# A hybrid SSD / HGRN2 / MoE layer on one core: an output-clearing store issued earlier, and the last pass's matmuls in another order

## The chip, the cores and the metric

The kernel runs on one core of one Trainium2 chip. Its time is the device time of one execution, in microseconds (us). TensorE (PE), VectorE (DVE), ScalarE (ACT) and GpSimd (POOL) compute; SyncE (SP) runs nearly all transfers of the stages looked at here from one queue, in the order in which its program issues them.

## The reference

One layer of a diffusion backbone on 512 latent and 256 context tokens of width 1024, in float32. Cut to the parts that the change lies in:

```
mixed = sigmoid(gm) * (ys @ w_branch_ssm) + sigmoid(gh) * (oh @ w_branch_hg)    # "merge"
mix   = mixed @ w_out
xl    = xl + gt1 * rms_norm(mix, g_post_mix)
h     = rms_norm(xl, g_pre_ffn) * (1 + sc2) + sh2
...                                # top-1 of 4 groups, then top-2 of its 8 experts, for each token
y[t]  = sum over its two experts e:  w_e * ((silu(h @ w_gate[e]) * (h @ w_up[e])) @ w_down[e])
out   = xl + gt2 * rms_norm(y, g_post_ffn)
```

ys and oh are the outputs of the two token mixers (a Mamba-2 scan and an HGRN2 scan), which the kernel computes before all of this.

## The kernel before

The five engines run programs of their own, tied by semaphores. The work has stages in this order: the modulation of the inputs, the SSD mixer, the HGRN2 mixer, the merge, the routing, the experts. The order in each engine's program is written by hand; a `wait_ge` holds that engine, and all that stands behind it in its program, until a semaphore has reached a count.

**Merge.** A loop over eight column tiles j of 128. For each tile PE computes two gates (lines of `merge_gate`, L1352), the SSM branch (L1758, 16 matmuls of 128x512) and the HGRN2 branch (L1760, 8 matmuls). A float32 matmul shows as two MATMUL instructions in the profile. The weights of tile j are 2.5 MB in four loads (two of gates at L1702, L1703, L1704) into one of two buffers r = j % 2. For j of 2 and more, SP issues them in `load(j, r)` after `s_brp >= j - 1`, and behind them 2 MB of modulation weights (`terms`, L1694), from which DVE makes one row a tile (`modulation_terms`, L1906, L1908). PE begins a tile with

```python
pe.wait_ge(s_wm[r], t * 64 + 32 + 32 * r)
```

so all four loads of the tile must have landed. Each finished row goes to DRAM by a small store from ACT (L1838), and SP waits for that (`s_modst`, L1707) before it loads the next bias (L1697). `w_out`, 4 MB, is loaded at L1732, ahead of the loop.

**Clearing y_dram.** Each expert writes its rows by an indirect store to `y_dram` (1024 rows of 1024 floats, 4 MB), of which all rows are first set to zero: POOL clears a 128x1024 tile `no_rows` (L2055) after the first mixed tile, and SP sends it to all of `y_dram` in one store (L1739), which before stands behind the loop over tiles. The first expert weights wait for that store (L2329, `s_cleared`), since they overwrite `no_rows`.

**After the merge.** SP waits for the last tile and for its stored row (L2299), then loads vectors, `x` and the router's weights (from L2310), then the first experts' weights. PE multiplies by `w_out` (L1776) and turns and routes the tokens.

**Experts.** Passes of two experts with 64 token slots each: gate and up (`up`, L2537), a turn of the product (L2544), down (`down`, L2555), copied by DVE (L2682, L2683) and stored by POOL (L2413). Weights of 4 MB a chunk stream into four homes. The last pass is written out by itself. Its result isn't stored, but added on PE to what the earlier passes stored: SP loads `y_dram` back in two halves (L2394), `s_yl`; DVE adds each token's two rows for the four chunks cc of 128 tokens (L2700, L2701), `s_fa`; `stored_choices(cc)` (L2630) puts chunk cc into its two PSUM banks (2 matmuls, 4 instructions); and `last_choices(cc, hf)` (L2633) adds the last pass's rows from `yb[0]`. The weights of the down projection come in four parts, `down_part(f)` (L2642, 4 matmuls, 8 instructions). SP issues parts 0 and 1 ahead of the loads from `y_dram`, and parts 2 and 3 behind them (L2287). After the last part DVE and ACT copy the two banks of the down projection into `yb[0]` (L2705, L2505), and only then can `last_choices(0, 0)` begin. ACT and DVE then normalise the chunks one by one (L2508 to L2513, L2711, L2715), and SP stores them (L2401).

Of the kernel before, what the change touches and what calls it, by code (L numbers as in the profile page):

```python
# [14 lines left out]
P = 128  # L15
D = 1024
# [5 lines left out]
LCH = LAT // P  # L22
# [38 lines left out]
FT = FF // P  # L61
# [5 lines left out]
PASSES = STEPS + 1  # L67
# [39 lines left out]
def build(nc, x, c, ctx, c_ctx, w_ada, b_ada, g_pre_mix, g_post_mix, g_pre_ffn, g_post_ffn, w_in,  # L107
# [7 lines left out]
    with es:  # L115
# [3 lines left out]
        def sem(name):  # L119
            return es.enter_context(nc.semaphore(name))  # L120
# [1557 lines left out]
        y_dram = nc.dram_tensor("y_dram", (2 * LAT, D), F32, kind="Internal").ap()  # L1678

        no_rows = arena[:, 6144:6144 + D]  # L1680

        def merge_sync(sp):

            def gate_source(j, b):
                return w_in_t[:, :, bass.ds((OFF_GM, OFF_GH)[b] + j * P, P)]

            def ssm_source(j):
                return wbs_t[:, :, bass.ds(j * P, P)]

            def hg_source(j):  # L1690
                return wbh_t[:, :, bass.ds(j * P, P)]

            def terms(j):
                sp.dma_start(wada2, w_ada_t[:, :, bass.ds(2 * D + j * 512, 512)]).then_inc(s_aw, 16)  # L1694

            def bias(j):
                sp.dma_start(adaw[0:1, :], b_ada[:, bass.ds(2 * D + j * 512, 512)]).then_inc(s_ab, 16)  # L1697

            def load(j, r):
                sp.wait_ge(s_brp, j - 1)  # L1700
                for b in range(2):
                    sp.dma_start(wmg[r][:, 8 * b:8 * b + 8, :], gate_source(j, b)).then_inc(s_wm[r], 16)  # L1702
                sp.dma_start(wmb[r][:, 0:16, :], ssm_source(j)).then_inc(s_wm[r], 16)  # L1703
                sp.dma_start(wmb[r][:, 16:24, :], hg_source(j)).then_inc(s_wm[r], 16)  # L1704
                sp.wait_ge(s_ac, j)
                terms(j)
                sp.wait_ge(s_modst, 16 * j)  # L1707
                bias(j)

            last = 8 * (HH - 1)  # L1710
            for b in range(2):
                sp.wait_ge(s_pu, last + 2 + 2 * b)
                sp.dma_start(wmg[0][:, 8 * b:8 * b + 8, :], gate_source(0, b)).then_inc(s_wg1, 16)
            sp.wait_ge(s_pu, last + 6)
            sp.dma_start(wmb[0][:, 0:16, :], ssm_source(0)).then_inc(s_wm[0], 16)
            sp.wait_ge(s_pu, last + 7)
            terms(0)
            sp.wait_ge(s_pu, last + 8)
            sp.dma_start(wmb[0][:, 16:24, :], hg_source(0)).then_inc(s_wm[0], 16)
            sp.wait_ge(s_sg, 4 * HH - 2)  # L1720
            sp.dma_start(wmg[1][:, 0:8, :], gate_source(1, 0)).then_inc(s_wm[1], 16)
            sp.wait_ge(s_q, HH)
            sp.dma_start(wmg[1][:, 8:16, :], gate_source(1, 1)).then_inc(s_wm[1], 16)
            sp.wait_ge(s_kdT, START + HH)
            bias(0)
            sp.wait_ge(s_out, START + HH)
            sp.dma_start(wmb[1][:, 0:16, :], ssm_source(1)).then_inc(s_wm[1], 16)
            sp.dma_start(wmb[1][:, 16:24, :], hg_source(1)).then_inc(s_wm[1], 16)
            sp.wait_ge(s_ac, 1)
            terms(1)  # L1730
            sp.wait_ge(s_ohd, START + HH)
            sp.dma_start(wout, w_out[0].rearrange("(k p) n -> p k n", p=P)).then_inc(s_wout, 16)  # L1732
            sp.wait_ge(s_modst, 16)
            bias(1)
            with sp.Fori(1, KT // 2) as t:
                for r in range(2):
                    load(t * 2 + r, r)
            sp.wait_ge(s_iota, ROWS_CLEAR)
            sp.dma_start(y_dram.rearrange("(j p) d -> p j d", p=P),  # L1739
                         no_rows.unsqueeze(1).broadcast_to([P, 2 * LCH, D])).then_inc(s_cleared, 16)  # L1740

        def merge_tensor(pe):
            def pair(t, warm):
# [276 lines left out]
        s_iota = sem("index_rows_ready")  # L2020
# [7 lines left out]
        s_gu = sem("gated_ready")  # L2028
        s_gut = sem("gated_transposed")
        s_guc = sem("gated_columns_ready")  # L2030
        s_d = sem("down_projected")
# [7 lines left out]
        ROWS_CLEAR, INDEX_ROWS, ROWS_NUMBERED = 1, 2, 3  # L2039
        s_part = {1: [s_wg1, s_wout, s_xres], 2: [s_aw, s_ab, s_modst]}  # L2040
        PART_BASE = {1: [32, 16, 16], 2: [128, 128, 128]}
        s_cleared = s_gc
# [210 lines left out]
        def weights_of(chunk):  # L2253
            w = home(chunk).rearrange("p (u q) -> p u q", u=2)
            if chunk % 3 == 2:
                return [w[:, u, :].rearrange("p (k n) -> p k n", n=D) for u in range(2)]
            return [w[:, u, :].rearrange("p (k f) -> p k f", f=FF) for u in range(2)]
# [257 lines left out]
        def experts_tensor(pe):  # L2515
# [9 lines left out]
            def part_landed(kind, part):  # L2525
                if part:
                    pe.wait_ge(s_part[kind][part - 1], PART_BASE[kind][part - 1] + 32)
# [34 lines left out]
            for step in STEP:  # L2562
                p = FIRST_PASS[step]
# [38 lines left out]
            n = pe.value_load(npair[0:1, 0:1], min_val=1, max_val=NOV // 2 + 1)  # L2602
# [13 lines left out]
            for cc in range(LCH):  # L2616
                mm = pe.transpose(bank[7][:, cc * P:(cc + 1) * P], cT[:, cc, :], ident[:, :])
# [9 lines left out]
            def stored_choices(cc):  # L2627
                pe.wait_ge(s_fa, cc + 1)
                for hf in range(2):
                    pe.matmul(bank[OUT_BANK[cc][hf]][:, :], ident[:, :], ylc[:, cc, hf * 512:(hf + 1) * 512], start=True, stop=False)  # L2630

            def last_choices(cc, hf):
                pe.matmul(bank[OUT_BANK[cc][hf]][:, :], cS[:, cc * P:(cc + 1) * P], yb[0][:, hf * 512:(hf + 1) * 512],  # L2633
                          start=False, stop=True).then_inc(s_fp, 1)

            def down_part(f):
                part_landed(2, f)
                w = weights_of(FINAL + 2)
                for hf in range(2):
                    for u in range(2):  # L2640
                        cols = slice(u * SLOT, (u + 1) * SLOT)
                        mm = pe.matmul(bank[5 + hf][cols, :], guT[:, f, cols], w[u][:, f, hf * 512:(hf + 1) * 512],  # L2642
                                       start=(f == 0), stop=(f == FT - 1))
                return mm

            pe.wait_ge(s_guc, PASSES + n + 1)
            pe.wait_ge(s_yb, PASSES + n)
            pe.wait_ge(s_w[(FINAL + 2) % 4], landed(OVER + 1) + n * 32)
            down_part(0)
            down_part(1)  # L2650
            pe.wait_ge(s_gu, PASSES + n + 1)
            stored_choices(0)
            stored_choices(1)
            down_part(2)
            down_part(3).then_inc(s_d, 1)
            stored_choices(2)
            pe.wait_ge(s_yb, PASSES + n + 1)
            last_choices(0, 0)
            pe.wait_ge(s_guc, PASSES + n + 2)
# [61 lines left out]
        @block.sync  # L2721
        def _(sp):
            modulate_sync(sp)
            ssd_sync(sp)
            hg_sync(sp)
            merge_sync(sp)
            experts_sync(sp)
# [24 lines left out]
        @block.tensor  # L2752
        def _(pe):
            for s in (s_xp, s_zp, s_kv, s_yd, s_yo, s_yt, s_kdT, s_la, s_kvH, s_out):
                pe.sem_inc(s, START)
            modulate_tensor(pe)
            ssd_tensor(pe)
            hg_tensor(pe)
            merge_tensor(pe)
            route_tensor(pe)  # L2760
            experts_tensor(pe)
# [41 lines left out]
```

## Time and profile before

| | us |
|---|---|
| median of 3 runs | 1880.98 |
| lowest, highest | 1880.73, 1887.57 |
| the profiled execution, its own time | 1887.57 |
| its span, first to last instruction | 1885.8 |

Times in the profile count from the start of the span. Busy time of PE counts MATMULs; a busy PE may be at half its clock, which is the column PEclk (1.00 is 2.4 GHz, 0.50 is 1.2 GHz). DMA share is the mean busy share of 16 DMA engines. A merged row of the timeline has a start, a length, an engine, a line and a count of instructions; in square brackets stands the idle time before it, and what ended it.

### The profile page before, as it was taken

Reading aid. Unit: us, or ns where it says so; the run is one execution under the profiler, and the core shown is the slowest. Engines: PE = TensorE matmul, PEld = TensorE weight load, DVE = VectorE, ACT = ScalarE, POOL = GpSimd, SP = SyncE. Lnnn points to the kernel's source line nnn. Section 1 sums busy time; section 2 is a strip of 40 time slices with the busy share of each in tenths; the row PEclk is TensorE's granted clock in tenths of the full one; section 3 lists DMA queues with packets and bytes.
Section 4 is the critical chain, followed back from the end, with each engine's and each line's share of the span. In section 5 each row is a group of like instructions: output and inputs, shape, how many; then the busy total and the mean of one; then the engine's idle time right before and its main releaser. Section 6 shows DMA issues by size and latency. Waiting matters only on the chain.

```text
span 1885.8 us, 19064 instructions
## 1 busy us (share of the span) xinstructions
PE 1766.8 (94%) x7112; PEld 957.6 (51%) x7112; DVE 717.5 (38%) x1176; ACT 486.3 (26%) x853; POOL 395.1 (21%) x472
## 2 busy tenths in 40 slices
PE   5999999999999999999999999999888987988877
PEld 2555555655556777767776444444533332333332
DVE  4526446364467555645646411311340000000004
ACT  3221422314134344344442100001311010111012
POOL 2024142231445433344333000000000000010000
PEclk9999999999999999999999999999889989999999
DMA  7221323113221111111120853344669999999996
GB/s 298 94 83 51 112 67 130 50 45 97 78 71 34 45 45 44 44 44 33 46 94 27 293 175 100 120 170 140 266 270 419 429 431 430 428 376 429 430 426 248
DMA packets 153578, 340.06 MB, mean 180 GB/s; under 512 B 15318, under 2 KB 105647, under 8 KB 140714
## 3 DMA queue, kind: packets, MB, share of 16 engines
q1 hardware_dynamic: 135648, 315.26, 43.9%
q10 hardware_dynamic: 13114, 15.89, 2.5%
q0 software_dynamic: 4752, 8.05, 1.1%
q8 instruction: 41, 0.67, 0.1%
q14 instruction: 23, 0.19, 0.0%
HBM read 331.44 MB, written 16.99 MB: 185 GB/s over the span
## 4 chain that ended last, share of the span: by engine, by line
PE 84%; DMA 7%; issue 3%; DVE 3%; ACT 1%; SPq 1%; POOL 0%; DVEq 0%; POOLq 0%; ACTq 0%
PE bank L774 12%; PE bank L522 12%; PE bank L2537 9%; PE bank L815 6%; PE bank L2555 5%; PE bank L1758 5%; PE bank L527 5%; PE bank L1352 4%; DMA arena<-in_w_up_dram 3%; PE bank L1776 3%; PE bank L518 3%; PE bank L1760 3%; PE bank L1386 3%; DMA arena<-in_w_down_dram 2%; PE bank L859 2%
## 5 line engine op out<-in xcount | busy, mean ns | idle before, releaser
L774 PE MATMUL bank<-stay,arena 128*128 128x512 f32 (+1 forms) x704 | 240.0, 497 | 0.0
L2537 PE MATMUL bank<-arena 128*64 128x512 f32 x832 | 189.6, 613 | 18.8 <-DMA arena<-in_w_up_dram 8.9
L774 PEld LDWEIGHTS bank<-stay,arena 128*128 128x128 f32 x704 | 132.4, 190 | 99.7 <-issue 92.3
L522 PE MATMUL bank<-arena 128*128 128x512 f32 x384 | 168.9, 593 | 0.0
L1256 POOL TENSOR_TENSOR arena<-arena 128x256 f32<-128x256 f32 x112 | 87.8, 784 | 267.8 <-DVE arena L1509 153.7
L2555 PE MATMUL bank<-arena 128*64 128x512 f32 x416 | 105.7, 666 | 33.6 <-issue 15.8
L2537 PEld LDWEIGHTS bank<-arena 128*64 128x64 f32 x832 | 66.8, 141 | 137.0 <-issue 120.5
L815 PE MATMUL bank<-arena,stay 128*128 128x512 f32 x256 | 114.6, 596 | 3.0 <-DVE arena L1067 3.0
L522 PEld LDWEIGHTS bank<-arena 128*128 128x128 f32 x384 | 71.7, 190 | 83.7 <-issue 83.7
L2676 DVE TENSOR_TENSOR arena<-arena,bank 128x512 f32<-128x512 f32 x17 | 11.7, 687 | 238.9 <-PE bank L2537 238.9
L1528 DVE TENSOR_TENSOR arena<-arena 128x256 f32<-128x256 f32 x112 | 58.9, 566 | 104.5 <-ACT arena L1287 73.0
L1758 PE MATMUL bank<-stay,arena 128*128 128x512 f32 x224 | 97.4, 593 | 0.0
L2413 POOL DMA_INDIRECT y_dram<-arena x16 | 16.1, 1007 | 384.9 <-DVE arena L2683 384.3
L534 ACT COPY arena<-bank 128x512 f32<-128x512 f32 x64 | 32.4, 506 | 213.2 <-PE bank L522 93.7
L575 POOL TENSOR_TENSOR arena<-arena,tok 128x512 f32<-128x512 f32 x40 | 49.5, 1241 | 173.0 <-ACT arena L654 109.9
L2444 ACT ACTIVATE arena<-bank,arena 128x128 f32<-128x128 f32 x136 | 49.2, 467 | 137.5 <-PE bank L2522 136.2
L2555 PEld LDWEIGHTS bank<-arena 128*64 128x64 f32 x416 | 37.5, 151 | 92.8 <-issue 88.6
L1352 PE MATMUL bank<-stay,arena 128*128 128x512 f32 x192 | 84.0, 595 | 0.0
L2682 DVE COPY arena<-bank 128x512 f32<-128x512 f32 x16 | 11.1, 691 | 187.5 <-PE bank L2555 187.5
L1258 POOL TENSOR_TENSOR arena<-arena 128x256 f32<-128x256 f32 x112 | 80.5, 719 | 0.0
L815 PEld LDWEIGHTS bank<-arena,stay 128*128 128x128 f32 x256 | 47.3, 190 | 61.2 <-issue 51.7
L1922 DVE TENSOR_TENSOR stay<-stay,bank 128x512 f32<-128x512 f32 x8 | 5.5, 687 | 180.6 <-PE bank L1760 180.6
(432 smaller groups left out, 2733.0 us busy)
## 6 DMA issues: line engine op xcount, KB each, us to landing
arena<-in_w_gate_dram SPq DMA_DIRECT2D x24, 2048.0 KB, 17.7
arena<-in_w_down_dram SPq DMA_DIRECT2D x24, 2048.0 KB, 22.7
arena<-in_w_up_dram SPq DMA_DIRECT2D x22, 2048.0 KB, 22.2
arena<-in_w_in_dram SPq DMA_DIRECT2D x58, 512.0 KB, 3.8
arena<-in_w_ada_dram SPq DMA_DIRECT2D x12, 2048.0 KB, 10.3
stay<-in_w_gate_dram SPq DMA_DIRECT2D x8, 2048.0 KB, 21.4
stay<-in_w_up_dram SPq DMA_DIRECT2D x8, 2048.0 KB, 17.3
arena<-in_w_in_dram ACTq DMA_DIRECT2D x6, 2048.0 KB, 9.7
```

The lines of the kernel that those rows point to most:

```text
L518: mm = pe.matmul(b[:, 0:CTX], w[:, k, :], hT[:, k, LAT:T], start=(k == 0), stop=(k == KT - 1))
L522: mm = pe.matmul(b[:, :], w[:, k, :], src[:, k, 0:LAT], start=(k == 0), stop=(k == KT - 1))
L527: mm = pe.matmul(b[:, i * P:(i + 1) * P], lhs, w[:, k, :], start=(k == 0), stop=(k == KT - 1))
L774: mm = pe.matmul(ps[:, 0:n], w[:, k, :], hT[:, k, o:o + n], start=(k == 0), stop=(k == KT - 1))
L815: mm = pe.matmul(bank[z_bank(j)][:, :], hT[:, k, j * P:(j + 1) * P], wz[:, k, :], start=(k == 0), stop=(k == KT - 1))
L1256: pool.tensor_tensor(first[:, :, 0:half], one, two, ALU.subtract)
L1258: ins = pool.tensor_tensor(second[:, :, half:], one, two, ALU.subtract)
L1352: mm = pe.matmul(bank[4 * r + b][:, :], wmg[r][:, 8 * b + k, :], hT[:, k, 0:LAT], start=(k == 0), stop=(k == KT - 1))
L1528: own.mark(dve.tensor_tensor(wv[:, :, s], ev[:, :, s], level_view(kh[d], half)[:, :, s], ALU.mult))
L1758: pe.matmul(bank[4 * r + 2][:, :], wmb[r][:, k, :], ysT[:, k, :], start=(k == 0), stop=(k == 15))
L2537: mm = pe.matmul(b[cols, :], xgT[r][:, k, cols], w[u][:, k, :], start=(k == 0), stop=(k == KT - 1))
L2555: mm = pe.matmul(bank[5 + hf][cols, :], guT[:, f, cols], w[u][:, f, hf * 512:(hf + 1) * 512], start=(f == 0), stop=(f == FT - 1))
```

## The change

Two places. In `merge_sync` the store that clears `y_dram`, with its wait for `no_rows`, is issued before the loads of tiles 2 to 7 instead of behind them. In the last expert pass on PE, `stored_choices(0)` and `(1)` now come ahead of the first down part, `stored_choices(2)` comes between down part 0 and down part 1, and parts 1 to 3 follow one another.

```diff
             bias(1)
+            sp.wait_ge(s_iota, ROWS_CLEAR)
+            sp.dma_start(y_dram.rearrange("(j p) d -> p j d", p=P),
+                         no_rows.unsqueeze(1).broadcast_to([P, 2 * LCH, D])).then_inc(s_cleared, 16)
             with sp.Fori(1, KT // 2) as t:
                 for r in range(2):
                     load(t * 2 + r, r)
-            sp.wait_ge(s_iota, ROWS_CLEAR)
-            sp.dma_start(y_dram.rearrange("(j p) d -> p j d", p=P),
-                         no_rows.unsqueeze(1).broadcast_to([P, 2 * LCH, D])).then_inc(s_cleared, 16)
...
+            stored_choices(0)
+            pe.wait_ge(s_gu, PASSES + n + 1)
+            stored_choices(1)
             pe.wait_ge(s_guc, PASSES + n + 1)
             pe.wait_ge(s_yb, PASSES + n)
             pe.wait_ge(s_w[(FINAL + 2) % 4], landed(OVER + 1) + n * 32)
             down_part(0)
-            down_part(1)
-            pe.wait_ge(s_gu, PASSES + n + 1)
-            stored_choices(0)
-            stored_choices(1)
-            down_part(2)
-            down_part(3).then_inc(s_d, 1)
             stored_choices(2)
+            for f in range(1, FT):
+                mm = down_part(f)
+            mm.then_inc(s_d, 1)
             pe.wait_ge(s_yb, PASSES + n + 1)
             last_choices(0, 0)
```

## Rows read from the trace of the kernel before

**Rows 1.** Windows: share of PE, DVE, ACT, POOL, clock and DMA by stretch.

```profile
800.00:1000.00 200.00, 200.00 (x1057) 143.02 (x1057) 110.73 (x183) 83.78 (x121) 85.68 (x112) 1.00 0.20 58
1400.00:1500.00 100.00, 88.14 (x396) 36.13 (x396) 7.90 (x12) 15.28 (x39) 8.13 (x8) 0.93 1.00 425
```

**Rows 2.** The chain that ended last, merge and what follows it.

```profile
1075.86 13.93 PE bank L1352 x32
...
1280.92 6.88 PE bank L1760 x16
...
1290.76 27.70 PE bank L1776 x64
```

**Rows 3.** Timeline of SP's transfers in the merge.

```profile
1058.76 0.25 SPq L1697 DMA_DIRECT2D arena<-in_b_ada_dram  x1
1059.37 1.01 SPq L1702 DMA_DIRECT2D arena<-in_w_in_dram  x2
...
1061.68 2.88 SPq L1704 DMA_DIRECT2D arena<-in_w_branch_hg_dram  x1
...
1256.99 0.38 SPq L1739 DMA_DIRECT2D y_dram<-arena  x1
1291.98 0.36 SPq L2310 DMA_DIRECT2D stay<-modrows  x1
```

**Rows 4.** Timeline of POOL, where the tile of zeros is made.

```profile
1055.34 1.24 POOL L2055 MEMSET arena<- 128x1024 f32 x1 [32.60 <-DVE arena L1924]
```

**Rows 5.** Windows of 2 us: the last columns are PEclk, DMA share and GB/s.

```profile
1058.00:1060.00 2.00, 2.00 (x6) 0.95 (x5) 1.93 (x3) 0.00 (x0) 0.00 (x0) 1.00 0.28 111
1064.00:1066.00 2.00, 2.00 (x6) 0.95 (x5) 0.00 (x0) 0.00 (x0) 0.00 (x0) 1.00 1.15 347
1258.00:1260.00 2.00, 2.00 (x6) 0.95 (x5) 1.91 (x3) 0.00 (x0) 0.00 (x0) 1.00 1.02 422
1514.00:1516.00 2.00, 2.00 (x7) 0.64 (x5) 0.00 (x0) 0.00 (x0) 0.00 (x0) 0.53 0.98 418
```

**Rows 6.** Transfers: count, KB each, us from issue to landing.

```profile
y_dram<-arena SPq DMA_DIRECT2D x1, 4096.0 KB, 11.4
arena<-in_w_branch_hg_dram SPq DMA_DIRECT2D x8, 512.0 KB, 7.5
```

**Rows 7.** Timeline of PE in the last pass.

```profile
1851.45 0.72 PE L2544 MATMUL bank<-ident,arena 128*128 128x128 f32 x4 [0.95 <-DVE arena L2676]
1852.90 3.65 PE L2642 MATMUL bank<-stay,arena 128*64 128x512 f32 x16 [0.73 <-ACT arena L2454]
1857.95 3.88 PE L2630 MATMUL bank<-arena,ident 128*128 128x512 f32 x8 [1.39 <-DVE arena L2701]
1863.23 1.94 PE L2642 MATMUL bank<-stay,arena 128*64 128x512 f32 x8 [1.41 <-DMA stay<-in_w_down_dram]
1865.71 1.94 PE L2642 MATMUL bank<-stay,arena 128*64 128x512 f32 x8 [0.54 <-DMA stay<-in_w_down_dram]
1867.58 1.98 PE L2630 MATMUL bank<-arena,ident 128*128 128x512 f32 x4
1869.40 5.31 PE L2633 MATMUL bank<-arena,stay 128*128 128x512 f32 x12
```

**Rows 8.** Timeline of DVE in the last pass.

```profile
1858.50 1.28 DVE L2701 SCALAR_TENSOR_TENSOR arena<-arena 128x1024 f32<-128x1024 f32 x1
1861.55 1.28 DVE L2701 SCALAR_TENSOR_TENSOR arena<-arena 128x1024 f32<-128x1024 f32 x1
1867.70 0.69 DVE L2705 COPY arena<-bank 128x512 f32<-128x512 f32 x1 [2.89 <-PE bank L2642]
```

**Rows 9.** Timeline of PE in the passes: matmuls after an idle stretch.

```profile
1513.31 8.78 PE L2555 MATMUL bank<-arena 128*64 128x512 f32 x32 [2.98 <-ACT arena L2454]
1573.80 7.09 PE L2555 MATMUL bank<-arena 128*64 128x512 f32 x32 [2.98 <-ACT arena L2454]
1836.55 13.95 PE L2537 MATMUL bank<-arena 128*64 128x512 f32 x64 [2.55 <-ACT arena L2444]
```

## The prediction

> **What bounds the kernel now.** I read the windows first. Before the routing PE is the bound: in a stretch of two hundred microseconds of the mixers it is busy for all of them, DMA at 0.20 [rows 1]. In the experts the transfers are: share 1.00, 425 GB/s, PE at 88 of 100 us [rows 1]. So a delay that reaches PE before the experts delays the start of the weight stream, and with it the end, one for one; a delay inside the stream would be hidden; and one behind the last weights counts in full again. The change has one edit in the first kind of place, and one in the last.
>
> The chain that ended last shows the merge: from tile 2 (1075.86) to the end of tile 7 (1280.92 + 6.88 = 1287.80) it is PE alone, six tiles in 211.94 us, 35.3 us each, with no wait for a load in it [rows 2]. The reader is to see there that every microsecond in which PE waits for a tile's weights is a new one. Then SP's timeline: the store that clears y_dram goes at 1256.99, and SP's next transfer, held by the last tile, at 1291.98 [rows 3]. Last, the timelines of the final pass [rows 7, 8].
>
> **The store: what it is taken from.** It lands 11.4 us after its issue [rows 6], at 1268.4, and nothing is issued until 1291.98 [rows 3]: its cover is 23.6 us of empty queue. The first expert weights wait for it only after that. So taking it out there gives 0 us. If that cover were gone, it would give up to 11.4 us.
>
> **The store: what it is put in front of.** In the new place SP comes to it right after the bias load at 1058.76 [rows 3]. Its own wait is for the zeros, done at 1055.34 + 1.24 = 1056.58 [rows 4]: no new wait on SP. Its issue costs SP 0.38 us [rows 3]. What is queued behind it is the whole of tile 2: 2.5 MB of weights, issued from 1059.37 to 1061.68 + 2.88 [rows 3], then 2 MB of modulation weights. In the kernel before, the queue has just run dry there (share 0.28 in 1058 to 1060 [rows 5]), so tile 2's data start about 1060.5, run at 347 GB/s [rows 5] and are complete 7.5 us after the start of the last issue, 1061.68 + 7.5 = 1069.2 [rows 3, 6]. PE begins tile 2 at 1075.86 [rows 2]. So tile 2 has a slack of 6.7 us, and the store must fit into it.
>
> It does not. 4.19 MB at 422 GB/s, the rate of the same store where it stands now [rows 5], are 9.9 us. Starting about 1060.0, they leave the queue's engines free at about 1069.9, where tile 2's data would have started at 1060.5: a shift of 9.4 us. Tile 2 then lands at 1069.2 + 9.4 = 1078.6 and PE, ready at 1075.86, waits **2.7 us**. Bounds: if half of the 1.2 us between issue and first data overlaps, 2.1; if tile 2's data start only when the store has landed whole, 11.4 us after an issue at 1059.3, the shift is 1070.7 - 1059.4 = 11.3 and the wait 4.6 us. I take 2.7: a DMA share of 1.00 over 100 us of one load after another [rows 1] says that this queue goes from one transfer to the next without a gap.
>
> The Trainium skill (DMA: Bandwidth & Descriptors, "Specifications") gives an HBM limit of some 358 GB/s for a core; by it the store would take 11.7 us (an estimate from that page) and the wait would be 4.5 us. The store's own row, 422 GB/s, contradicts it here, and I go by the row.
>
> What else is behind the store: DVE's modulation row of tile 2 starts some 6 us later (its weights follow tile 2's on the queue), but PE wants it only at the end of tile 2, about 35 us on. SP may issue tile 3's loads when PE has done tile 1, about 1075.9; if they take the 9.8 us of tile 2's (1059.37 to 1069.2) they land near 1086 and are wanted at 1075.86 + 35.3 = 1111.2, so 9.4 us later is still early. So there is one stall, and by tile 3 the queue has caught up. What is late next is all that follows on PE: w_out's matmuls at 1290.76, the vectors at 1291.98, routing, the start of the stream. Nothing there has slack against PE, so 2.7 us pass to the end.
>
> Does the stall lower the clock? Rows 9 show what idling does: the same 32 instructions take 8.78 us after 2.98 us of idle time in one pass (clock 0.53 just behind it [rows 5]) and 7.09 in another, so a drop costs 1.7 us and comes after most but not all gaps near 3 us. The gap of 2.55 us left the next matmuls at full speed [rows 9]. For 2.7 us I expect no drop (0 us; the other end is 1.7).
>
> **The last pass on PE.** In the kernel before, down parts 0 and 1 run from 1852.90 for 3.65 us, while the rows from y_dram are still on their way; `stored_choices(0)` begins at 1857.95, when DVE has added the first chunk [rows 7]. Parts 2 and 3 wait for their weights, and part 3 begins at 1865.71 and ends at 1867.65. Then DVE and ACT copy for 0.69 us [rows 8], hidden under `stored_choices(2)` (1867.58, 1.98 us), and `last_choices(0, 0)` begins at 1869.40 [rows 7].
>
> After the change PE reaches `stored_choices(0)` at 1852.17 (1851.45 + 0.72) and stands behind it until 1857.95, because nothing about the rows from y_dram is earlier. The 3.65 us of parts 0 and 1 have lost their cover. From there PE is alone the bound, instruction by instruction. An instruction of 128x512 takes 0.43 us (1.94 us for 4 and their drain, of which about 0.22 is drain: 1.72), and one of a down part half of that (8 in 1.72), as two run side by side:
>
> - `stored_choices(0)`: 1857.95 to 1859.67
> - `stored_choices(1)`: its chunk is ready at 1858.50 + 1.28 = 1859.78 [rows 8], so 1859.88 to 1861.60
> - down part 0: to 1863.32
> - `stored_choices(2)`: its chunk is ready at 1862.83 [rows 8], so to 1865.04
> - down parts 1, 2, 3: 5.15 us to 1870.19, plus the drain, 1870.4. Part 3's weights are there from 1865.71 [rows 7], so it waits for none.
> - the copies of 0.69 us, now with nothing over them, and 0.2 us of hand-over: `last_choices(0, 0)` at **1871.3**, against 1869.40: 1.9 us later.
>
> From `last_choices(0, 0)` on nothing changes: ACT and DVE do the four chunks in the same order, and DVE sets the end.
>
> Then the clock. PE now idles from 1852.17 to 1857.95, 5.8 us, twice what in most passes was enough for a drop. At the full price of 1.7 us, of which some 0.2 goes into the wait for the second chunk that PE had anyway, this is 1.5 us. Ends: 0, and 2.9 (the 5.8 us gap could hold the low clock over more work: half of the whole wait). I take 1.5. The sum for the last pass is **3.4 us**, between 1.9 and 4.8.
>
> **Sum.** 0 + 2.7 + 0 + 1.9 + 1.5 = 6.1 us slower, bounds 2.1 + 1.9 = 4.0 and 4.6 + 1.7 + 4.8 = 11.1. Against the profiled execution's own 1887.57 us (span 1885.8, so 1.8 us around it) this is 1893.7. That execution was the slowest of the three; the same 6.1 us on the median of 1880.98 give **1887.1 us**, 0.32% slower. A measurement of this kernel tells about 0.5%, 9.4 us, from no change; the runs before alone spread over 6.8 us.
>
> **Rivals.**
>
> *A. Slower by more than 0.5%: tile 2 waits until the store has landed.* Place: the start of tile 2. It decides when loads behind a store in one queue wait for its completion, or when SP is held in issuing them. Then PE waits 4.6 us, a gap after which a clock drop is near certain, 1.7; with 3.4 in the last pass 9.7 us, 1890.7. Against it: the queue streams loads without gaps; for it: the trace shows no store with loads right behind it. Chance 0.15. The Trainium skill (same page, "Anatomy of one DMA") puts most of a fixed 2 us of a transfer into the receipt of its last write, longest for HBM; it says this of the semaphore, not of the data behind it, and no row here shows which holds.
>
> *B. Faster: the stored chunks fill waits.* The order pays if PE's work is done when part 3's weights arrive: `stored_choices(2)` would be out of the 1.98 us behind part 3 [rows 7], of which 0.9 is needed for copies anyway, so at most 1.1 us are won. PE has 5.15 us of down parts from 1865.04, and would have to begin them 2.8 us earlier, so the rows from y_dram would have to come 2.8 us earlier. With a hidden store the time would be 1879.9; with more than 0.5% faster only if the move of the store also frees something at 1292, where the queue is empty. Chance 0.04, most of it measurement.
>
> *C. The merge edit is hidden.* If the store and tile 2 share the engines better than first come, first served, or tile 2's slack is larger than 6.7 us, only the last pass pays: 3.4 us, 1884.4; without a clock drop 1.9, 1882.9. Chance 0.20.
>
> **Chances.** The forecast 0.61, A 0.15, B 0.04, C 0.20. The likeliest is 1887.1. The range takes C without a drop and a little of the spread below, and A with the upper bounds: 1881.0 to 1892.5. Of the forecast's cases one in ten crosses 9.4 us with the spread, of A's half or more: slower 0.17; faster 0.03; within 0.80.
>
> **What would show it.** In the profile after: the clearing store at about 1059.3; an idle gap of PE of 2 to 3 us ahead of L1352 of tile 2, released by a load; tiles 3 to 7 without one; nothing new between 1287 and 1320 but the shift; in the last pass an idle gap of 5 to 6 us ahead of the first L2630, a clock at 0.5 behind it, and 1.9 to 3.4 us more from the landing of the rows of y_dram to the first L2633. The forecast is wrong if that first gap isn't there, if it is over 4 us, or if the stream of weights swallows the delay.

## The result

| | before | after |
|---|---|---|
| median, us | 1880.86 (4 runs) | 1894.01 (4 runs) |
| lowest to highest | 1879.78 to 1887.57 | 1893.01 to 1895.22 |
| span of the profiled execution | 1885.8 | 1891.7 |

The ratio is 1.0062, with a 95% interval of 1.0038 to 1.0087: the change makes the kernel slower, by 13.2 us on these medians. Put on 1880.9 us, the ratio is 11.7 us and its interval 7.1 to 16.4. The forecast was 6.1 us slower, 1887.1 us, with a range up to 1892.5; the direction was right and the time lies outside.

SP's timeline of the kernel after, in the merge, answers to [rows 3]:

```profile
1057.26 0.24 SPq L1697 DMA_DIRECT2D arena<-in_b_ada_dram  x1
1057.55 0.37 SPq L1736 DMA_DIRECT2D y_dram<-arena  x1
1058.29 8.43 SPq L1702 DMA_DIRECT2D arena<-in_w_in_dram  x2
1066.91 3.10 SPq L1703 DMA_DIRECT2D arena<-in_w_branch_ssm_dram  x1
1070.10 2.88 SPq L1704 DMA_DIRECT2D arena<-in_w_branch_hg_dram  x1
```

The store is the transfer right behind the bias load, as forecast (at 1057.55, where 1059.3 was named). What is new is the second column: SP needs 8.43 us to issue two loads that took it 1.01 before [rows 3], and the last load of tile 2 is issued 12.6 us after the store. PE's timeline there, and the windows (PEclk, DMA share and GB/s last):

```profile
1073.49 1.02 PE L1766 MATMUL bank<-arena,ones 128*1 128x512 f32 x2
1077.85 15.67 PE L1352 MATMUL bank<-stay,arena 128*128 128x512 f32 x32 [3.35 <-DMA arena<-in_w_branch_hg_dram]
...
1115.00 14.00 PE L1352 MATMUL bank<-stay,arena 128*128 128x512 f32 x32
```

```profile
1068.00:1070.00 2.00, 2.00 (x6) 0.80 (x6) 0.00 (x0) 0.00 (x0) 0.00 (x0) 1.00 0.91 222
1070.00:1072.00 2.00, 2.00 (x6) 0.91 (x5) 0.00 (x0) 0.00 (x0) 0.00 (x0) 1.00 1.15 347
1080.00:1082.00 2.00, 2.00 (x4) 0.86 (x3) 0.00 (x0) 0.00 (x0) 0.00 (x0) 0.50 1.05 410
```

A new idle gap of 3.35 us stands ahead of tile 2, and the 32 instructions behind it take 15.67 us where tile 3's take 14.00: the clock is at 0.50, and that costs 1.7 us more. From tile 3 on nothing waits. In the chain that ended last, the gap ends with the landing of tile 2's last load, and SP's own issuing is a link ahead of it:

```profile
1066.91 3.10 SPq L1703
...
1070.10 7.52 DMA arena<-in_w_branch_hg_dram
...
1077.85 4.16 PE bank L1352 x6
```

A link in that chain doesn't say yet what SP's being held costs. For that I set the two profiles side by side, counted from SP's issue of the bias load. Tile 2's last load landed 10.42 us after it in before (1058.76 to 1069.18) and 20.36 us after it in after (1057.26 to 1070.10 + 7.52 = 1077.62): 9.9 us more, where the forecast had 9.4. So whatever the forecast lacked there, SP's being held included, costs 0.5 us in all.

Whether the loads wait for the store to land can be read from the packets: those of the store are of 4 KB, those of the loads under 2 KB. The first line is of the kernel before, for 1265.5 to 1267.5, two us near the end of its store. The other two are of the kernel after, for 1067 to 1069 and for 1069 to 1070.05, which is the moment at which the store has landed (1057.55 + 12.5):

```profile
DMA packets 208, 0.85 MB, mean 426 GB/s; under 512 B 0, under 2 KB 0, under 8 KB 208
```

```profile
DMA packets 136, 0.56 MB, mean 279 GB/s; under 512 B 0, under 2 KB 0, under 8 KB 136
DMA packets 416, 0.27 MB, mean 257 GB/s; under 512 B 16, under 2 KB 398, under 8 KB 416
```

The loads' packets run before the store has landed, so they don't wait for that. But with loads queued behind it the store's own last packets are slower (279 GB/s where it had 426), and it lands 12.5 us after its issue where it took 11.4. Why, no run here shows.

The last pass on PE answers to [rows 7], and DVE's row to [rows 8]:

```profile
1855.81 0.72 PE L2544 MATMUL bank<-ident,arena 128*128 128x128 f32 x4 [0.95 <-DVE arena L2676]
1859.08 6.25 PE L2630 MATMUL bank<-arena,ident 128*128 128x512 f32 x8 [2.55 <-DVE arena L2701]
1865.26 1.94 PE L2642 MATMUL bank<-stay,arena 128*64 128x512 f32 x8
1867.12 1.98 PE L2630 MATMUL bank<-arena,ident 128*128 128x512 f32 x4
1869.04 5.37 PE L2642 MATMUL bank<-stay,arena 128*64 128x512 f32 x24
1875.20 5.42 PE L2633 MATMUL bank<-arena,stay 128*128 128x512 f32 x12 [0.79 <-DVE arena L2705]
```

```profile
1856.95 0.75 DVE L2700 TENSOR_SCALAR arena<-arena 128x1024 f32<-128x1024 f32 x1 [1.29 <-DMA arena<-y_dram]
...
1874.46 0.69 DVE L2705 COPY arena<-bank 128x512 f32<-128x512 f32 x1 [8.43 <-PE bank L2642]
```

PE idles ahead of `stored_choices(0)`, whose instructions, eight together with those of `(1)`, then take 6.25 us (3.88 before), works through all down parts, and stands for the copies, 0.79 us, which lay under a matmul before.

To see what each stretch costs I cut every profiled execution at the same five starts: the first L1760 of the merge, the first L1776, the first L2537, the first L2700, the first L2633, and the end of the span (the lines shift by a few in some of the variants). Differences of these, in us, for all kernels that were run:

| kernel | up to the merge | merge | w_out, routing | experts | last pass | end | span |
|---|---|---|---|---|---|---|---|
| before | 1046.03 | 244.73 | 93.77 | 471.20 | 13.67 | 16.40 | 1885.8 |
| before again (e1) | 1042.34 | 244.74 | 93.86 | 469.47 | 13.73 | 16.36 | 1880.5 |
| after | 1044.67 | 249.82 | 92.36 | 470.10 | 18.25 | 16.50 | 1891.7 |
| e2 store only | 1043.51 | 250.75 | 93.82 | 471.85 | 13.67 | 16.40 | 1890.0 |
| e3 last pass only | 1043.44 | 244.73 | 93.88 | 470.29 | 17.40 | 16.46 | 1886.2 |
| e4 both | 1042.91 | 249.96 | 92.15 | 470.09 | 17.65 | 16.54 | 1889.3 |
| e5 two stores | 1045.50 | 260.82 | 92.15 | 469.82 | 13.66 | 16.45 | 1898.4 |
| e6 two halves | 1046.66 | 244.73 | 92.16 | 469.70 | 13.71 | 16.44 | 1883.4 |
| e7 behind tile 3 | 1045.08 | 244.73 | 92.18 | 470.15 | 13.67 | 16.39 | 1882.2 |
| e8 filled waits | 1045.55 | 248.46 | 93.83 | 470.61 | 17.91 | 16.54 | 1892.9 |
| e9 stored ahead | 1046.88 | 244.73 | 92.15 | 470.24 | 13.52 | 16.48 | 1884.0 |
| e10 parts late | 1044.94 | 244.73 | 93.90 | 469.65 | 14.87 | 16.41 | 1884.5 |

The merge and the last pass repeat to 0.1 us when nothing in them is changed. Those are the only two stretches in which after differs from before beyond what executions of one kernel differ by: +5.1 and +4.6 us, 9.7 in sum. What the change doesn't touch varies by itself: 1042.3 to 1046.9 up to the merge, 92.2 or 93.8 in the routing, 469.5 to 471.9 in the experts.

### The profile page after: what moved, and what is told of

Read it like the earlier page. It is cut to its first block, busy times and chain, and to the rows that moved or that the text cites. A ratio compares the mean times of both kernels' runs of the same rounds, so it can differ in the third digit from the quotient of the medians.

```text
span 1891.7 us, 19064 instructions
## 1 busy us (share of the span) xinstructions
PE 1771.4 (94%) x7112; PEld 959.5 (51%) x7112; DVE 717.3 (38%) x1176; ACT 486.6 (26%) x853; POOL 395.7 (21%) x472
## 4 chain that ended last, share of the span: by engine, by line
PE 84%; DMA 7%; issue 3%; DVE 3%; ACT 2%; SPq 1%; ACTq 0%; POOL 0%; DVEq 0%; POOLq 0%
PE bank L774 12%; PE bank L522 12%; PE bank L2537 9%; PE bank L815 6%; PE bank L2555 5%; PE bank L527 5%; PE bank L1352 5%; PE bank L1758 4%; PE bank L1776 3%; PE bank L518 3%; PE bank L1386 3%; PE bank L1760 3%; DMA stay<-in_w_up_dram 2%; DMA stay<-in_w_down_dram 2%; PE bank L859 2%
## 5 line engine op out<-in xcount | busy, mean ns | idle before, releaser
L2537 PE MATMUL bank<-arena 128*64 128x512 f32 x832 | 186.8, 606 | 15.2 <-ACT arena L2444 7.6
L2537 PEld LDWEIGHTS bank<-arena 128*64 128x64 f32 x832 | 66.2, 140 | 131.2 <-issue 118.0
L2676 DVE TENSOR_TENSOR arena<-arena,bank 128x512 f32<-128x512 f32 x17 | 11.7, 688 | 238.3 <-PE bank L2537 238.3
L1352 PE MATMUL bank<-stay,arena 128*128 128x512 f32 x192 | 85.7, 605 | 3.3 <-DMA arena<-in_w_branch_hg_dram 3.3
```

The costliest lines, as they stand in the source:

```text
L1352: mm = pe.matmul(bank[4 * r + b][:, :], wmg[r][:, 8 * b + k, :], hT[:, k, 0:LAT], start=(k == 0), stop=(k == KT - 1))
L2537: mm = pe.matmul(b[cols, :], xgT[r][:, k, cols], w[u][:, k, :], start=(k == 0), stop=(k == KT - 1))
```

## Experiments

**e1, the kernel before once more**, to see what its own executions do.

> The kernel before, unchanged. Theory: its profiled execution of 1887.57 us was not typical; a new one takes 1880 to 1882 us, and the 6 to 7 us less lie in the experts (from the start of the first expert pass at L2537 to the load of y_dram), not in the merge or the last pass. Rival: the 6.8 us are spread evenly or lie ahead of the merge, and then the profile of before can be used as it stands. Ratio to before 1.000, within 0.003.

Measured 1882.52 us (11 runs, 1880.22 to 1885.21) beside 1884.03 for 27 runs of before on the same chip (1880.17 to 1887.12); ratio 0.9994, 0.9985 to 1.0003. The expectation of where the difference sits was wrong: of the 5.3 us between the two spans 3.7 lie ahead of the merge and 1.7 in the experts. 1887 us isn't an odd execution but the upper end of a spread of 7 us. So the four runs of before with their median of 1880.86 were low for this kernel: 27, 23 and 23 runs of it in three later comparisons have medians of 1884.03, 1884.47 and 1884.64.

**e2, e3, e4: each edit alone, and both.** e2 takes only the hunk of `merge_sync`, e3 only that of the last pass, e4 is the changed kernel. The additions, cut (the same lines are taken out at their old places):

```diff
 e2
+            sp.wait_ge(s_iota, ROWS_CLEAR)
+            sp.dma_start(y_dram...).then_inc(s_cleared, 16)
             with sp.Fori(1, KT // 2) as t:
 e3
+            stored_choices(0)
+            stored_choices(1)
             down_part(0)
+            stored_choices(2)
...
```

> Only the store is moved, the last pass is as before. Theory: PE waits 3.3 us ahead of tile 2 and then runs 3.4 us at half clock, 1.7 us more: 5.0 us, and all of it passes to the end: 1885.9 us. Rival (the stream of weights swallows part of it): 0 to 3 us. Rival (the early store has a second cost in the experts, which the two profiles don't show): 8 us or more.

> Only the order of the last pass on PE is changed, the store is where it was. Theory: from the rows of y_dram to the first L2633 4.6 us more, as in the profile of after against before: 1885.5 us. Rival (as predicted, 1.9 in instructions and 1.5 of clock): 3.4 us, 1884.3. Rival (the parts of the measured 13.2 us that the merge doesn't explain are here): 8 us.

> The changed kernel again, as the sum to which the two single edits are held. Theory: 5.0 + 4.6 = 9.6 us plus at most 1 to 2 of interplay, 1890.5 to 1892.5 us. Rival: the two edits act on each other (another clock phase, a longer wait) and the sum of the single ones falls short of both together by over 3 us: 1894.

| | median, us (runs) | ratio to before, 95% | the ratio put on 1884.03, us |
|---|---|---|---|
| e2 store only | 1889.06 (11) | 1.0022, 1.0013 to 1.0031 | +4.1 |
| e3 last pass only | 1887.95 (11) | 1.0021, 1.0012 to 1.0030 | +4.0 |
| e4 both | 1892.84 (5) | 1.0049, 1.0035 to 1.0063 | +9.2 |

The last column goes by the ratio; the medians themselves differ by 5.0, 3.9 and 8.8 us. Each edit alone costs about 4 to 5 us, and the two add up to that of both within the intervals. So the times show no effect of one on the other, and the three theories (5.0, 4.6 and 9.6 us) lie within the intervals. For e3 the interval (2.3 to 5.7 us) also contains the rival's 3.4; its profile has 3.7. In the profiles the merge costs 6.0 in e2 and 5.2 in e4, the last pass 3.7 in e3 and 4.0 in e4 (e2's profiled execution is the longest of its eleven). PE's rows of e2 and of e3:

```profile
1077.81 15.48 PE L1352 MATMUL bank<-stay,arena 128*128 128x512 f32 x32 [4.47 <-DMA arena<-in_w_branch_hg_dram]
```

```profile
1854.47 5.40 PE L2630 MATMUL bank<-arena,ident 128*128 128x512 f32 x8 [2.68 <-DVE arena L2701]
```

e2's gap is 1.1 us longer than that of after, though from the store's issue to tile 2's start it is 20.3 us in both (1057.52 to 1077.81, and 1057.55 to 1077.85). The difference is when SP comes to the store: it stands behind the small store of a modulation row, and that let SP go on 6.7 us after PE's first L1766 in e2 (1050.57 to 1057.23) and 5.5 in after (1051.74 to 1057.26).

**e5, a second store behind the first**, to a spare tensor. The count that the first expert weights wait for is raised to match, here and in e6.

```diff
             sp.dma_start(y_dram...).then_inc(s_cleared, 16)
+            sp.dma_start(spare_dram.rearrange("(j p) d -> p j d", p=P),
+                         no_rows.unsqueeze(1).broadcast_to([P, 2 * LCH, D])).then_inc(s_cleared, 16)
             with sp.Fori(1, KT // 2) as t:
```

> The store moved as in e2, and a second one of the same 4 MB of zeros right behind it, to a spare DRAM tensor that nothing reads; the last pass as before. Theory (one queue, in order, so what lies ahead of tile 2 adds to its wait in full): the idle gap ahead of tile 2 grows by the second store's 9.9 us, from 3.3 to 4.5 us to 13 to 15 us, with again one drop of the clock; 1899 us. Rival (the loads wait until a store has landed): 11.4 us or more are added, 16 us or more. Rival (stores and loads overlap): under 8 us are added.

Measured 1899.83 us (4 runs), ratio 1.0084, 1.0066 to 1.0102. SP's rows and PE's:

```profile
1059.44 0.37 SPq L1737 DMA_DIRECT2D y_dram<-arena  x1
1059.85 0.58 SPq L1739 DMA_DIRECT2D spare_dram<-arena  x1
1060.81 17.53 SPq L1703 DMA_DIRECT2D arena<-in_w_in_dram  x2
```

```profile
1089.55 15.80 PE L1352 MATMUL bank<-stay,arena 128*128 128x512 f32 x32 [14.22 <-DMA arena<-in_w_branch_hg_dram]
```

From the first store's issue to tile 2's start it is 30.1 us, 9.8 more than with one store; 4.19 MB at 422 GB/s are 9.9. A store ahead in the queue adds its data time to what waits behind it. This alone doesn't refute the rival that loads wait for a store to land: the second store needn't wait for the first one's landing, so by that rival too it would add only its data time. The packets of after refute it. SP is held for it too: 17.53 us for the two loads. The clock drops once, as with a gap of 3.35 us, and costs 1.8.

**e6, the store in two halves**, one ahead of tile 2's loads, one ahead of tile 3's.

```diff
+            sp.dma_start(y_dram...[:, 0:LCH, :], ...).then_inc(s_cleared, 16)
+            load(2, 0)
+            sp.dma_start(y_dram...[:, LCH:2 * LCH, :], ...).then_inc(s_cleared, 16)
+            load(3, 1)
+            with sp.Fori(2, KT // 2) as t:
```

> The store is cut into two of 2 MB: one ahead of tile 2's loads, one ahead of tile 3's; tiles 4 to 7 in the loop as before; the last pass as before. Theory (tile 2 has 6.7 us of slack, a half takes 5.0 us, tile 3 has over 20 us): no idle gap of PE ahead of tile 2 or tile 3, or one of under 0.5 us, no drop of the clock there, and the time of before. Rival (any store ahead of tile 2 holds SP in issuing its loads): a gap of 1.5 us or more. Rival (the place of the store costs by itself later on, in the experts): as slow as e2.

Measured 1884.44 us (12 runs) beside 1884.47 of before (23 runs), ratio 1.0002, 0.9994 to 1.0011. The merge takes 244.73 us, as before. PE's rows, without a gap:

```profile
1075.47 1.02 PE L1771 MATMUL bank<-arena,ones 128*1 128x512 f32 x2
1076.42 14.00 PE L1352 MATMUL bank<-stay,arena 128*128 128x512 f32 x32
```

So 5.0 us of store fit into tile 2's slack of 6.7 us and 9.9 don't. Tile 2's last load, issued at 1067.37, lands 7.6 us later at about 1075.0, 1.5 us before PE wants it. SP is held here too (3.75 us for the two loads at L1702), and it costs nothing.

**e7, the whole store behind tile 3's loads.**

```diff
+            for r in range(2):
+                load(2 + r, r)
+            sp.wait_ge(s_iota, ROWS_CLEAR)
+            sp.dma_start(y_dram...).then_inc(s_cleared, 16)
+            with sp.Fori(2, KT // 2) as t:
```

> The whole store in front of tile 4's loads and behind tile 3's; the last pass as before. Theory: it falls where tile 4 has over 20 us of slack; no gap, the time of before within 0.1%. Rival (the early store is bad anywhere in the loop): 4 us slower, as in e2. Rival (taking the store out of the end of the merge gives something): 1 us or more faster.

Measured 1884.79 us (12 runs), ratio 1.0003, 0.9993 to 1.0012. In the profile the merge is 244.73 us again, so neither being early nor being inside the loop costs anything, and having left the end of the merge gives nothing:

```profile
1114.26 0.37 SPq L1738 DMA_DIRECT2D y_dram<-arena  x1
1115.00 7.68 SPq L1702 DMA_DIRECT2D arena<-in_w_in_dram  x2
```

**e8, both edits with the waits filled.** Filler matmuls whose results are overwritten keep PE busy.

```diff
             pair(0, False)
+            pe.wait_ge(s_mx, 1)
+            for _ in range(4):
+                pe.matmul(bank[0][:, :], ident[:, :], ysT[:, 0, :], start=True, stop=True)
             with pe.Fori(1, KT // 2) as t:
...
+            pe.wait_ge(s_yb, PASSES + n)
+            for _ in range(6):
+                pe.matmul(bank[5][:, :], ident[:, :], row_keep[:, 0:512], start=True, stop=True)
             stored_choices(0)
```

> Both edits of the change, and filler matmuls of 128x512 by the identity whose results are overwritten: 4 (3.4 us) ahead of tile 2, 6 (5.2 us) ahead of the first stored_choices. The waits stay, but PE doesn't idle in them. Theory (a part of the cost is the half clock behind each gap): L1352 of tile 2 takes 14.0 us again, so the merge costs 3.4 to 4.5 us instead of 5.1 to 6.0; the first eight L2630 take 3.9 us, and from the rows of y_dram to the first L2633 15.6 us instead of 17.4 to 18.3, against 13.7 before; in all 3 to 4 us faster than both edits without filler, so about 1888.5 to 1889.5 us. Rival (the matmuls are slow there for another cause, such as the transfers): no change in these rows, or slower.

Measured 1892.24 us (6 runs), ratio 1.0042, 1.0026 to 1.0058: in the time it isn't the 3 to 4 us that I expected. The rows say why:

```profile
1079.07 13.97 PE L1352 MATMUL bank<-stay,arena 128*128 128x512 f32 x32
...
1857.74 5.32 PE L2651 MATMUL bank<-stay,ident 128*128 128x512 f32 x12
1862.89 3.60 PE L2633 MATMUL bank<-arena,ident 128*128 128x512 f32 x8
1866.42 1.94 PE L2645 MATMUL bank<-stay,arena 128*64 128x512 f32 x8
```

Both groups run at full clock: tile 2's L1352 in 13.97 us where it had 15.5 to 15.8, the eight instructions of `stored_choices` in 3.60 where they had 5.4 to 6.3. The merge costs 248.46 - 244.73 = 3.7 us, the bare wait. But the six fillers of the last pass were too many: in this execution DVE's first chunk was ready at 1859.24 + 1.29 = 1860.53, and PE was busy with filler until 1862.89. Not all of these 2.4 us count, since the second chunk was ready only at 1861.22 + 1.28 = 1862.50. What the excess cost can be told with e10 (below), where PE has the same two chunks ahead of the down parts and the clock stays up: there the parts begin 6.03 us after DVE's first L2699, here 1866.42 - 1858.45 = 7.97 us after DVE's first row. So 1.94 us are excess filler, and without them the last pass would be 17.91 - 1.94 = 15.97 us (an estimate from these rows), 2.3 more than before. A filler of fixed length doesn't fit a wait that varies.

**e9 and e10, the last pass taken apart.** e9 moves only `stored_choices(2)`, and keeps parts 0 and 1 first; e10 moves the parts, and keeps `stored_choices(2)` last.

```diff
 e9
             stored_choices(1)
+            stored_choices(2)
             down_part(2)
             down_part(3).then_inc(s_d, 1)
-            stored_choices(2)
 e10
             stored_choices(0)
             stored_choices(1)
+            for f in range(FT):
+                mm = down_part(f)
+            mm.then_inc(s_d, 1)
             stored_choices(2)
```

> The store where it was before; in the last pass down parts 0 and 1 stay first, as before, and only stored_choices(2) is moved, ahead of down parts 2 and 3. Theory (the cost of the new order is in parts 0 and 1 having lost their cover, and the move of stored_choices(2) by itself uncovers the copies but fills the wait for part 2): from the rows of y_dram to the first L2633 13.4 to 13.9 us, against 13.7 before; the time of before. Rival (the exposed copies are the cost): 14.5 us or more.

> The store where it was before; in the last pass all four down parts come behind stored_choices(0) and (1), but stored_choices(2) stays behind part 3, as before. Theory: the lost cover and the clock are here, only the exposed copies (0.9 us) are not, so 16.4 to 17.3 us from the rows of y_dram to the first L2633, against 17.4 to 18.3 with the whole edit, and an idle gap of 2.5 to 4 us ahead of stored_choices(0) with half clock behind it. Rival (the order of stored_choices(2) matters more): under 15 us.

e9: 1883.66 us (12 runs), ratio 0.9998, 0.9988 to 1.0007; the last pass 13.52 us. e10: 1887.53 us (10 runs), ratio 1.0017, 1.0008 to 1.0026; the last pass 14.87 us. PE's rows of e9, then of e10, with DVE's first row of e10 at the end:

```profile
1861.16 1.99 PE L2630 MATMUL bank<-arena,ident 128*128 128x512 f32 x4 [1.06 <-DVE arena L2701]
1863.07 3.65 PE L2642 MATMUL bank<-stay,arena 128*64 128x512 f32 x16
1867.52 5.42 PE L2633 MATMUL bank<-arena,stay 128*128 128x512 f32 x12 [0.79 <-DVE arena L2705]
```

```profile
1855.44 3.88 PE L2630 MATMUL bank<-arena,ident 128*128 128x512 f32 x8 [2.38 <-DVE arena L2700]
1859.25 7.09 PE L2642 MATMUL bank<-stay,arena 128*64 128x512 f32 x32
1853.22 0.75 DVE L2699 TENSOR_SCALAR arena<-arena 128x1024 f32<-128x1024 f32 x1 [1.03 <-DMA arena<-y_dram]
```

`stored_choices(2)` ahead of the parts is free: the exposed copies are paid by the wait for part 2 that it fills. In e10 the expectation of 16.4 to 17.3 us missed, and the number is that of its rival (under 15), for another reason: the gap was 2.38 us and no drop of the clock followed in the profiled execution. So it shows the price of the lost cover alone, 14.87 - 13.67 = 1.2 us; the 1.1 us from there to the 15.97 of e8 are the exposed copies. Its timed runs are 3 us above before, more than that; that the clock dropped in others of them is likely, and not shown.

## Why the prediction was wrong

**What bounds, and what the store frees: right.** Behind the empty queue at 1268 to 1292 the store cost nothing; e7 and e6 place it elsewhere in the loop and gain nothing.

**The wait ahead of tile 2: right in kind, sized too small.** The forecast was 2.7 us, the profiles show 3.35, 4.47 (e2) and 3.62 us (e4). Tile 2's slack lies between 5.0 and 9.9 us (e6, e2), and the second store of e5 adds its data time, as taken. In after, tile 2's data came 9.9 us later and not 9.4; the store's slower end is the likely cause, and that is argued, not shown. PE began 0.2 us after the landing (1077.62 to 1077.85), where I had put nothing. And I took SP's arrival at the store from one execution; it varies by over 1 us, all of it slack of tile 2, and that is the 1.1 us by which e2's gap is longer. Rival A had two conditions. That loads wait until the store has landed is refuted by the packets of after. That SP is held in issuing them is what happens, 8.43 us, but it didn't bring A's price: the shift was 9.9 us where A had 11.3, and e6 shows SP held at no cost.

**"I expect no drop" of the clock behind it: the step that failed.** Tile 2's first 32 instructions took 15.5 to 15.8 us in all four profiles with a gap (3.35, 3.62, 4.47, 14.22 us), and 14.0 in those without; filling the gap took the 1.7 us away (e8). I had argued from the gap of 2.55 us in [rows 9] that 2.7 would be harmless, and one row is no ground for that. The same gap stands ahead of the last L2537 in all twelve profiles (2.55 or 2.56 us), and in five of them the 64 instructions behind it took 15.65 us and not 13.95, the kernel before itself among them when it was run again (e1; then after, e4, e8, e10). Even the trace that I read has such a case after a shorter gap, where the first L2537 runs with the clock at 0.60 in 1384 to 1386:

```profile
1384.53 15.57 PE L2537 MATMUL bank<-arena 128*64 128x512 f32 x64 [1.94 <-ACT arena L2444]
```

With a gap already put at 2.1 to 4.6 us the drop was likelier than not, by the same rows: of gaps near 3 us most had one.

**The last pass: both terms right in kind, both somewhat small.** Lost cover and exposed copies were put at 1.9 us; by e8 and e10 they are 1.2 + 1.1 = 2.3. The clock was put at 1.5 us; e3, e4 and after have 17.40, 17.65 and 18.25 us, so 1.4, 1.7 and 2.3 above 15.97. The gap was put at 5.8 us and is 2.6 to 4 us in the profiles, since the rows from y_dram came 1.3 us after the last gated product in after where they came 4.4 us after it in the profile of before. 1.7 of these 3.1 us are again the clock, which was down for the last L2537 in after and not in before. The cost of the clock didn't follow the length of the gap (1.4 us behind 2.68, 1.7 behind 3.95, 2.3 behind 2.55); what it follows is not shown. That no wait for part 3 would remain was right.

**The sum and its base.** 6.1 us were forecast; the two stretches cost 9.7 us in the profiles. The 3.6 us between are 0.65 of the wait, 1.7 of the clock behind it, and 1.2 in the last pass. Five runs beside 27 of before (e4) give 9.2 us by the ratio, 8.8 by the medians. The measured 13.2 us are the difference of two medians of four runs; the interval of their ratio, 7.1 to 16.4 us, contains 9.2, and no experiment found a part of the change that costs more. The median of before that stood at the start, 1880.98 of three runs, is 3 to 4 us below what 73 later runs on three chips show. I had seen a spread of 6.8 us in three runs and still put the whole range on their median. With 9.2 us on 1884.0 the time would be 1893.2. That the forecast's other base, the slow profiled execution, gave 1893.7 beside the measured 1894.01 is luck: an increase too small on a base too high.

**Rivals B and C** didn't happen: no part of the change gains, and neither wait is hidden. What e9 shows of B is that its idea is sound only with parts 0 and 1 left in front: 0.15 us in the profile, and nothing that can be measured.

No version here beats the kernel before. If the store has to be early, e6 and e7 show two places where it is free.

## What to carry to other kernels

A transfer moved to an earlier place is charged, here by its data time, to the slack of what then stands behind it in the queue; compute that slack from the row of the load that lands last, and cut the transfer if it is too long. Work that is done during a wait is free only there: before moving something ahead of it, ask what stands under the wait afterwards. And price a new idle gap of PE of about 3 us with the half clock behind it: here that added 1.7 us to a wait of 3.4, and 1.4 to 2.3 us to an order that by itself cost 2.3. One gap that left the next matmuls fast is no ground to leave it out.

## What was not expected of the hardware

- SP isn't free once it has issued. Behind a store of 4 MB two loads of 512 KB kept it for 8.4 us, behind two stores for 17.5 us, behind 2 MB for 3.75 us, and 1.0 us with nothing ahead. What stands behind these loads in SP's program comes later by it: in after the last load of tile 2 is issued 12.6 us after the store.
- Executions of one kernel differ by 7 us (1880.2 to 1887.1 in 27 runs), and in the twelve profiles the part ahead of the merge alone varies by 4.5 us (1042.3 to 1046.9).
- A drop of the clock in a PE-bound stretch cost 1.5 to 1.8 us, whether the gap ahead of it was 3.35 us or 14.22 us.
- The same gap in the same place is followed by the low clock in one execution and not in the next: 5 of 12 at 2.55 us.
- A 4 MB store with loads queued behind it landed 12.5 us after its issue, 1.1 us later than with nothing behind it, and its last packets ran at 279 GB/s where they had 426.
